# TensorE multiplies ones into a spare bank inside nine norms

## The reference

```python
def layer_norm(x, g=None, b=None):
    mu = jnp.mean(xf, axis=-1, keepdims=True)
    var = jnp.mean(jnp.square(xf - mu), axis=-1, keepdims=True)
    y = (xf - mu) * lax.rsqrt(var + LN_EPS)
...
def rmsnorm(x, w):
    y = xf * lax.rsqrt(jnp.mean(xf * xf, axis=-1, keepdims=True) + EPS)
...
x = layer_norm(ALPHA * x + gate1 * token_mixer(layer_norm(x) * (1 + scale1) + shift1), ln1_g, ln1_b)
x = layer_norm(ALPHA * x + gate2 * channel_mixer(layer_norm(x) * (1 + scale2) + shift2), ln2_g, ln2_b)
```

## Time and profile before

| | us |
|---|---|
| median of three runs | 3597.31 (3596.95 to 3599.4) |
| span of the profiled execution | 3594.8 |
| median less that span | 2.5 |
| PE busy | 3327.1 (93% of the span) |
| DVE, ACT, POOL busy | 1702.4, 1181.5, 962.3 |
| matmul instructions | 17158 |

### The profile page before, as it was taken

How to read it: one execution, slowest core, us unless ns; L and a number is a source line. 1 busy time by engine, 2 the same in 40 slices (tenths; PEclk the granted TensorE clock), 3 DMA queues, 4 the chain that set the end, 5 groups by cost and what they waited for, 6 DMA issues and landing times. The chain is left out here.

```text
span 3594.8 us, 42433 instructions
## 1 busy us (share of the span) xinstructions
PE 3327.1 (93%) x17158; PEld 2642.7 (74%) x17158; DVE 1702.4 (47%) x2635; ACT 1181.5 (33%) x1920; POOL 962.3 (27%) x412
## 2 busy tenths in 40 slices
PE   5999989988999799999999777989999888899998
PEld 4887667866888688888888664368887664578887
DVE  6995467554332323355510897552211585653211
ACT  3223364324443422122231224333222323543222
POOL 0001322432444122322332110024444221024443
PEclk7999999998999899999999998989999888899999
DMA  4222324451223222333321000012233110023332
GB/s 188 99 97 86 130 99 154 154 176 59 95 98 93 74 88 84 128 135 131 134 73 57 30 18 7 1 65 94 95 111 96 48 52 27 1 65 94 100 94 88
DMA packets 91790, 315.99 MB, mean 88 GB/s; under 512 B 10822, under 2 KB 12614, under 8 KB 90314
## 3 DMA queue, kind: packets, MB, share of 16 engines
q1 hardware_dynamic: 88876, 304.74, 25.8%
q10 hardware_dynamic: 2720, 8.55, 0.6%
HBM read 311.16 MB, written 2.10 MB: 87 GB/s over the span
## 5 line engine op out<-in xcount | busy, mean ns | idle before, releaser
L261 POOL TENSOR_TENSOR terms<-streams,terms 128x1024 fp32r<-128x1024 f32 (+2 forms) x408 | 962.1, 2358 | 2613.1 <-ACT terms L249 2613.1
L519 PE MATMUL bank<-terms,terms 128*128 128x512 f32 (+2 forms) x3776 | 1407.5, 373 | 24.2 <-POOL terms L261 10.3
L520 PE MATMUL bank<-terms,terms 128*128 128x512 f32 (+2 forms) x3776 | 1401.9, 371 | 0.0
L521 PE MATMUL bank<-terms,terms 128*128 128x512 f32 (+2 forms) x3776 | 1400.4, 371 | 0.0
L249 ACT ACTIVATE terms<-streams 128x1024 fp32r<-128x1024 f32 (+1 forms) x462 | 475.5, 1029 | 1741.6 <-PE bank L521 1494.0
L519 PEld LDWEIGHTS bank<-terms,terms 128*128 128x128 f32 x3776 | 715.5, 189 | 159.5 <-issue 30.9
L521 PEld LDWEIGHTS bank<-terms,terms 128*128 128x128 f32 x3776 | 715.0, 189 | 121.9
L520 PEld LDWEIGHTS bank<-terms,terms 128*128 128x128 f32 x3776 | 716.1, 190 | 119.1
L1946 DVE TENSOR_TENSOR stage<-stage,bank 128x256 f32<-128x256 f32 (+1 forms) x84 | 51.8, 618 | 544.4 <-ACT stage L1924 544.4
L1319 DVE SCALAR_TENSOR_TENSOR arena<-arena,vec 128x512 f32<-128x512 f32 x240 | 162.5, 745 | 0.2
L1910 DVE TENSOR_TENSOR terms<-stage,terms 128x512 fp32r<-128x512 f32 (+1 forms) x66 | 114.3, 1735 | 0.0
(11 more groups left out here) (379 smaller groups left out, 3476.8 us busy)
## 6 DMA issues: line engine op xcount, KB each, us to landing
streams<-in_ffn_w SPq DMA_DIRECT2D x104, 512.0 KB, 3.5
streams<-in_w_mod SPq DMA_DIRECT2D x72, 512.0 KB, 3.6
streams<-in_w_up SPq DMA_DIRECT2D x44, 512.0 KB, 3.5
streams<-in_w_gu SPq DMA_DIRECT2D x44, 512.0 KB, 3.5
streams<-in_w_ada SPq DMA_DIRECT2D x32, 512.0 KB, 3.5
streams<-in_w_down SPq DMA_DIRECT2D x32, 512.0 KB, 3.5
streams<-in_w_v SPq DMA_DIRECT2D x24, 512.0 KB, 3.7
streams<-in_ffn_w SPq DMA_DIRECT2D x24, 384.0 KB, 3.3
```

The lines of the kernel that those rows point to most:

```text
L261: gp.tensor_tensor(self.low(m), self.raw(n), self.high(m), ALU.subtract).then_inc(self.low_made.sem, 1)
L519: pe.matmul(out, high[:, at], x_high, start=kk == start, stop=False)
L520: pe.matmul(out, high[:, at], x_low, start=False, stop=False)
L521: mm = pe.matmul(out, low[:, at], x_high, start=False, stop=kk == kts - 1)
```

## The change

A Norm takes `spare=(first, each, before, after)`. It then takes a third bank, and `turning(n)` multiplies a 128x128 tile of ones with itself into that bank n times. It is called with 1 behind the means and 5 behind their widening (norms with a mean only), with `each` between the tiles of `sums`, with `before` ahead of the wait for the reciprocal, and with `after` behind the widening; the last one frees the bank. The results are not read. Nine norms get it: the first one (which also turns 16 times before the tokens are there), ln1 and second of block one, ln2, the norm at the head of block two, its second one (`early`), its final one, the one at the head of block three, and the last. No other instruction changes, but the rotation of the banks moves by one behind each of these norms.

```diff
--- before.py
+++ after.py
@@ -660,8 +660,9 @@
 
 
     def __init__(self, k, src, whole, nt, n, mean, eps, center, gain=None, post=None, shift=None, parts=None,
-                 after=None, squared=None, early=None, ahead=None):
+                 after=None, squared=None, early=None, ahead=None, spare=None):
         self.k, self.src, self.whole, self.nt, self.n, self.center = k, src, whole, nt, n, center
+        self.spare = spare
         self.early, self.lows_last = early, False
         if early:
             squared = lambda j: early[j % len(early)]
@@ -672,6 +673,7 @@
         self.strip = n // 4
         self.mean_bank = k.take_bank() if center else None
         self.sum_bank = k.take_bank()
+        self.spare_bank = k.take_bank() if spare else None
         self.shifts = bool(post or shift)
         self.means = 1 if center else 0
         self.centred = nt if center else 0
@@ -706,15 +708,35 @@
         if self.ahead:
             self.ahead.tensor(pe, self)
             return
+        if self.spare is None:
+            self.sums(pe)
+            self.widened(pe)
+            return
+        first, each, before, after = self.spare
+        self.bank_there(pe, self.spare_bank)
+        if first:
+            self.turning(pe, first)
         if self.center:
             self.means_of(pe)
+            self.turning(pe, 1)
             self.means_widened(pe)
-        self.sums(pe)
+            self.turning(pe, 5)
+        self.sums(pe, each)
+        self.turning(pe, before)
         self.widened(pe)
+        self.turning(pe, after).then_inc(self.k.bank_free[self.spare_bank[0]].sem, 1)
 
     def bank_there(self, pe, of):
         if of[1]:
             pe.wait_ge(self.k.bank_free[of[0]].sem, of[1])
+
+    def turning(self, pe, n):
+
+
+        ones = self.k.mean[:, 3, :]
+        for _ in range(n):
+            mm = pe.matmul(self.k.bank[self.spare_bank[0]][:, :P], ones, ones, start=True, stop=True)
+        return mm
 
     def means_of(self, pe):
         k, nt = self.k, self.nt
@@ -730,7 +752,7 @@
         pe.wait_ge(*k.averaged(1))
         self.widen(pe, self.mean_bank, k.middle[:, :self.strip]).then_inc(k.spread.sem, 1)
 
-    def sums(self, pe):
+    def sums(self, pe, each=0):
         k, nt = self.k, self.nt
         self.bank_there(pe, self.sum_bank)
         for j in range(nt):
@@ -739,6 +761,8 @@
             else:
                 pe.wait_ge(*k.act_done(j + 1))
             self.by_strips(pe, self.sum_bank, self.squared(j), j == 0, j == nt - 1).then_inc(k.pe_done.sem, 1)
+            if each and j < nt - 1:
+                self.turning(pe, each)
 
     def widened(self, pe):
         k = self.k
@@ -1238,15 +1262,17 @@
 
 
     def __init__(self, k, whole, gain, shift, parts):
-        super().__init__(k, lambda j: k.X[:, j, :], whole, DT, SEQ, 0, LN_EPS, True, gain, None, shift, parts)
+        super().__init__(k, lambda j: k.X[:, j, :], whole, DT, SEQ, 0, LN_EPS, True, gain, None, shift, parts,
+                         spare=(0, 1, 30, 36))
         self.counts[k.gained] = 2
 
     def sync(self, sp):
         self.k.fetch_to(sp, self.k.dense_at[PARTED - 1])
 
     def tensor(self, pe):
+        pe.wait_ge(*self.k.constants(0))
+        self.turning(pe, 16)
         pe.wait_ge(*self.k.x_loaded(0))
-        pe.wait_ge(*self.k.constants(0))
         super().tensor(pe)
 
     def scalar(self, act):
@@ -2033,10 +2059,11 @@
     mixed = residual(k, "w_out", h_src, LAT_ONLY, lambda n, c: k.mod1[:, 16 + n:17 + n], ALPHA,
                      parted_before(k, DT), True)
     ln1 = Norm(k, lambda j: k.X[:, j, :], lambda j: k.X[:, j, :], DT, SEQ, 0, LN_EPS, True, lambda j: k.v("ln1_g", j),
-               None, lambda j: k.v("ln1_b", j), None, mixed.evicted)
+               None, lambda j: k.v("ln1_b", j), None, mixed.evicted, spare=(0, 1, 5, 5))
     centred = k.a(B1_HIDDEN, DT, SEQ)
     second = Norm(k, lambda j: k.X[:, j, :], lambda j: centred[:, j, :], DT, SEQ, 0, LN_EPS, True,
-                  lambda j: k.gain[:, 1, j:j + 1], None, lambda j: k.mod1[:, 24 + j:25 + j], h, ln1.ready)
+                  lambda j: k.gain[:, 1, j:j + 1], None, lambda j: k.mod1[:, 24 + j:25 + j], h, ln1.ready,
+                  spare=(0, 1, 5, 3))
     hidden = terms(k, B1_HIDDEN, B1_HIDDEN + FT * SEQ, FT, SEQ)
     up = conv_up(k, h_src, hidden, second)
     down = residual(k, "w_down", lambda kk, c: hidden(kk), LAT_ONLY, lambda n, c: k.mod1[:, 40 + n:41 + n], ALPHA,
@@ -2046,7 +2073,7 @@
 
 def block_one_end(k, after):
     return Norm(k, lambda j: k.X[:, j, :], lambda j: k.X[:, j, :], DT, SEQ, 0, LN_EPS, True, lambda j: k.v("ln2_g", j),
-                None, lambda j: k.v("ln2_b", j), None, after)
+                None, lambda j: k.v("ln2_b", j), None, after, spare=(0, 1, 5, 20))
 
 
 
@@ -2886,13 +2913,13 @@
     def stream(n, c):
         return k.X[:, n, :] if c else k.XC[:, n, :]
 
-    def modulated(m, at, c, after, whole, early=None):
+    def modulated(m, at, c, after, whole, early=None, spare=None):
 
         n = SEQ if c else CTX
         whole = k.a(whole, DT, n)
         return Norm(k, lambda j: stream(j, c), lambda j: whole[:, j, :], DT, n, 0, RMS_EPS, False,
                     lambda j: k.gain[:, at, j:j + 1], None, lambda j: k.mod2[:, m + j:m + j + 1, 1 - c],
-                    lambda j: src(j, c), after, None if c else lambda j: staged[:, CTX * j:CTX * (j + 1)], early)
+                    lambda j: src(j, c), after, None if c else lambda j: staged[:, CTX * j:CTX * (j + 1)], early, spare=spare)
 
     staged = k.stage[:, :, :, :].rearrange("p a b c -> p (a b c)")
 
@@ -2902,7 +2929,7 @@
     passes = before + [SecondGains(k, 16, 0, 16, ((0, 0), (1, 1)), ()),
                        Beside(k, down_one, ctx1, sums=4, squares=2, root=4, inverse=4, widened=5, shifted=5, scaling=5), VectorsAgain(k, down_one)]
     ln2 = block_one_end(k, down_one.evicted)
-    passes += [ln2, modulated(0, 0, 1, ln2.ready, B2_WHOLE)]
+    passes += [ln2, modulated(0, 0, 1, ln2.ready, B2_WHOLE, spare=(0, 1, 5, 3))]
     mod0 = passes[-1]
     squares = []
     for n, (a, b) in enumerate(((0, 11), (11, 22))):
@@ -2919,7 +2946,7 @@
     last = passes[-1]
     passes.append(SecondGains(k, 72, 24, 72, ((2, 0), (3, 1), (4, 0)), ((7, 64, 0),)))
     passes.append(behind(k, squares, modulated(24, 2, 1, lambda eng, j: last.evicted(eng, j, 1), B2_WHOLE,
-                                               staged_slots(k))))
+                                               staged_slots(k), (0, 0, 6, 3))))
     qg, fpre = k.a(B2_QG, 8, 512), k.a(B2_F, 8, TOK)
     of_queries = to_tiles(k, "w_qg2", lat_src, LAT_ONLY, ACT.Silu, lambda i, c: qg[:, i, :], paired=passes[-1])
     ctx2 = modulated(24, 3, 0, lambda eng, j: last.evicted(eng, j, 0), B2_WHOLE_CTX)
@@ -2957,7 +2984,8 @@
     slots = [k.arena[:, A_XC + 512 * j:A_XC + 512 * (j + 1)] for j in (1, 2, 3)] + [k.sq[:, j, :] for j in (1, 2, 0)]
     slots += [k.arena[:, at:at + 512] for at in (ARENA - 1040, ARENA - 528)]
     final = behind(k, of_down, Norm(k, lambda j: k.X[:, j, :], lambda j: k.X[:, j, :], DT, SEQ, 0, RMS_EPS, False,
-                                    lambda j: k.v("fnorm2", j), after=down.evicted, early=slots))
+                                    lambda j: k.v("fnorm2", j), after=down.evicted, early=slots,
+                                    spare=(0, 0, 5, 5)))
     return [first, heads, halves, out, third, up, LoadMeta(k), meta, final]
 
 
@@ -3520,7 +3548,7 @@
         return high[:, kk, s], low[:, kk, s]
     norm = Norm(k, lambda j: k.X[:, j, :], lambda j: whole[:, j, :], DT, SEQ, 0, RMS_EPS, False,
                 lambda j: k.v("attn_norm", j), parts=lambda j: (high[:, j, META:], low[:, j, META:]),
-                after=before[-1].ready)
+                after=before[-1].ready, spare=(0, 1, 5, 8))
     mixing = Mixing(k, src, norm.ready)
     selection = mixing.selection
     k.bank_set, k.bank_turn = [0, 1, 2, 3, 4], 0
@@ -3562,7 +3590,8 @@
     up = swiglu(k, "w_gu3", lambda kk, c: h(kk), LAT_ONLY, hidden, FT, middle, ahead)
     down = residual(k, "w_down3", lambda kk, c: hidden(kk), LAT_ONLY, None, 1.0, parted_before(k, FT), squares=of_down)
     final = behind(k, of_down, Norm(k, lambda j: k.X[:, j, :], lambda j: k.X[:, j, :], DT, SEQ, 0, RMS_EPS, False,
-                                    lambda j: k.v("fnorm3", j), after=down.evicted, early=staged_slots(k)))
+                                    lambda j: k.v("fnorm3", j), after=down.evicted, early=staged_slots(k),
+                                    spare=(0, 0, 5, 1)))
     return [halves, mixed, middle, up, down, final]
```

## The result

The changed kernel takes 3602.43 us (median of 20 runs), the kernel before 3597.02 us beside it: ratio 1.0014, 95% interval 1.0008 to 1.002. Some 5 us are lost where 4.9 were forecast to be won.

The account below looks back on a forecast made before the run. Dense passes were taken as bound by PE, norms as serial chains where TensorE waits. Gains 1.14 + 0.58 + 0.99 + 1.02 + 1.14 = 4.9 us gave 3592.4 us, 0.14% less; range 3588.6 to 3597.5.

Parts of the forecast that it names:

- price of the turn: In the norms, one turn was priced at 0.24 us at full clock or 0.445 us at half.
- price of the group: In the sums, one group was priced at 0.245 us at full clock (1.96 for eight), 0.49 at half.
- First norm: First norm: 95 turns, gain 0; upper bound of a loss 2 to 4 us if 36 turns ran at half.
- ln1: ln1 of block one: gain 0, both widenings already at full clock; turns before the widening fit with slack 0.45 us.
- second: second of block one: squares chain gains 1.14 us; means keep half clock, gain 0, upper bound 1.14.
- first rival: Second's means (1.14) and block three's first tile (1.05) also kept warm, perhaps ln1 (1.14): 3590.0 us or less; chance 0.29.
- ln2: ln2: first widening stays at half clock; second, 1.74 us against 1.16 at full clock, gains 0.58 us.
- Behind ln2: Norm behind ln2: tail 0.23, widening 0.81, context products 0.68 gained, three turns on the path cost 0.73; sum 0.99 us.
- the turns don't hold the clock, and run at half: Rival: a group with a turn takes 0.93 us at half clock; together +15 us, 3612; chance 0.05.
- The early norm: Early norm of block two: widening already at full clock; the sweep behind it starts its low products sooner, gaining 1.02 us.
- Block three: Norm at the head of block three: its squares chain ran at half clock; gain 1.14 us.
- first tile: Behind block three's head norm: paced by DVE without turns, expected at half clock again soon; gain 0, upper bound 1.05 us.

Follow-up runs that it names:

- two between: Two turns between the tiles of the sums where the changed kernel has one: 3608.23 us, 1.0025 of the kernel before.
- kernel with eight turns: The changed kernel with 8 turns in the first norm instead of 95: 3604.17 us, 1.0017 of the kernel before.
- kernel with nine turns in all: The changed kernel with only one turn in each of the nine norms, spare banks kept: 3592.37 us, 0.9997 of the kernel before.
- third look at the kernel before: The kernel before, run and profiled again without edit: single run of 3592.71 us, 156.1 us in the scans.
- best version: The changed kernel with turns in strips between squares and between second's means, and 30 turns behind ln2: 3595.64 us, 0.9988; again 3593.64 us, 0.999.

## Why the prediction was wrong

The step that failed is the cost of the turns between the squares. I wrote that `each` = 1 "about doubles TensorE's work in such a stretch" and charged nothing for it at full clock, without a sum. By my own prices a group of 0.245 us and a turn of 0.24 make 0.49, in an interval of 0.55 to 0.65, so I took it to be hidden. The price of the turn was right (0.22 from two between). The price of the group was taken from eight groups in a row, and does not hold between other shapes: 0.31 us more. With 0.775 us in place of 0.49 the interval is overrun, at seven gaps in five norms. (The first norm has seven such gaps too, hidden behind a later wait.) The rest of the mechanism held except in the norm behind ln2: elsewhere the clock was full in the squares, and the tails and widenings behind them shortened as priced.

Site by site, forecast against the changed kernel's first profile:

- First norm: 0 forecast, 0 found, by its own rows and by the kernel with eight turns.
- ln1: 0 forecast, 1.34 us lost. Seven gaps at 0.775 less 0.60 are 1.2 of it.
- second: 1.14 forecast for the tail of the squares and their widening. From the last group's first load to the scaling it took 3.10 us, as forecast. Its means, which I had left out as the upper bound, are at full clock in the changed kernel, as the first rival had it. But the gaps ate most of both: from the widening of the means to the scaling it is 11.21 us (817.90 to 829.11) against 11.94 before, so 0.73 won; from widening to widening 0.18 is lost.
- ln2: 0.58 forecast for the second widening. It is at full clock (1.16 us), but the chain ahead of it is 0.7 us longer.
- Behind ln2: 0.99 forecast with the three turns charged. With the 0.58 of ln2 that is a chain of 14.41 less 0.8; it was 19.09 with the clock fallen, 15.29 without. The rival "the turns don't hold the clock, and run at half" described this place, at 0.93 us a step; 1.31 was measured. I had it at 0.05, to decide once a third of the places are at half; one place at half and the full-clock overrun of the others, which no rival of mine had, did it.
- The early norm: 1.02 forecast, 1.22 found; against the other two profiles of the kernel before 0.3 and 1.0. All profiles with the six turns ahead of the widening have 11.56 to 11.59 us here. It has no turns between its groups.
- Block three: 1.14 forecast, 0.67 lost in the chain, the widening behind it 0.9 better. Its first tile falls back to half clock, as forecast.

Without the turns between, the forecast comes out where it was made: 4.6 us from ln1 to the scans, where the sum over these norms had 3.7. That the numbers are close is partly luck, for part of it is no gift of the turns. The kernel with nine turns in all had 1397.1 us there, and the third look at the kernel before 1396.8, and the clock's falls come at other moments in each run. What warm norms are worth there lies between 1.7 and 5.5 us by these profiles (1394.1 to 1395.1 against 1396.8 to 1399.6), and how much on average stays open; the two results of 0.9988 and 0.999 say about 4 us for the best version over the whole program, with intervals from under 1 to 8 us.

The range, 3588.6 to 3597.5, was also too narrow for a second reason. I put the spread of the runs at 0.5 us, though three runs had already spanned 2.45 us. The scans alone move by 8 to 10 us with the clock, and 20 runs of the kernel before span 3592.48 to 3604.16.

## What to carry to other kernels

Before filling TensorE's waits with work whose results nobody reads (filler), read the pace at which the awaited pieces come, and cost the filler with the shapes on either side of it: give it the shape and the column strips of its neighbours, or keep it out of loops that run at the pace of another engine. Filler in a single wait cost nothing here as long as it ended before the wait did. A few us in a program with stages that swing by 8 us with the clock can be read from the stages' own chains in the profile, and hardly from totals of ten runs.

## What the runs showed of the hardware

At full clock a product of 128x128 f32 (one call) costs 0.22 us among its like, a group of four calls in strips of 32 columns 0.22 to 0.245; one of each in turn costs 0.775 at full clock and 1.31 at half, not 0.46 and 0.93. TensorE can stand at half clock while the profile has it busy all the time: 6.90 us of 6.90 with 0.50 granted, in the alternation of the two shapes. The clock's falls within one stage go with 8 to 10 us between runs of one and the same kernel (154.4 and 156.1 us against 164.0 in its scans).
